# Gated linear attention inside a full decoder layer: the running sums of the gate made by a VectorE scan instead of fp32 products with a triangle of ones

## The reference, cut to what matters

```python
log_a = log_sigmoid((za @ w_gla_gate + b_gla_gate)) / 16        # (tokens, 4 heads * 128 channels)
# per chunk of tokens and per head:
cum = jnp.cumsum(gc, axis=-2)                                   # running sum of log_a over the tokens
o_inter = einsum('ik,kv->iv', qc * exp(cum), state)
attn    = (qc * exp(cum)) . (kc * exp(-cum)), causal            # written out with a decay in the reference
o_intra = einsum('ij,jv->iv', attn, vc)
state   = state * exp(last)[:, None] + (kc * exp(last - cum)).T @ vc
```

## Time and profile before

| | us |
|---|---|
| median of 3 runs | 2958.1 |
| the runs | 2984.66, 2958.1, 2953.07 |
| the profiled execution | 2954.94 |
| its span, slowest core (core 0) | 2953.4 |
| spans of the other cores | 2937.2 to 2952.8 |
| PE busy | 2800.8 (95%) |
| DVE busy | 1564.1 (53%) |
| ACT busy | 1341.3 (45%) |
| mean granted TensorE clock, core 0 | 0.986 |

### The profile page before, as it was taken

One profiled execution on the slowest core, in us unless ns is written; L12 is line 12 of the kernel. 1 busy time (PEld: TensorE's weight loads), 2 busy tenths in 40 slices (PEclk: granted clock), 3 DMA queues, 4 the chain that ended last, 5 costly groups with the idle time before them and its releaser, 6 DMA issues.

```text
span 2953.4 us, 47945 instructions; the slowest of 8 cores (2937.2 to 2953.4 us)
## 1 busy us (share of the span) xinstructions
PE 2800.8 (95%) x16320; PEld 1413.5 (48%) x16627; DVE 1564.1 (53%) x2490; ACT 1341.3 (45%) x2678; POOL 757.7 (26%) x980
## 2 busy tenths in 40 slices
PE   6999999997989997799999999999999999999998
PEld 2454455664545554344444455554444444444443
DVE  5887666664434443344454455445564554554643
ACT  4776565554665564222332265443442442433421
POOL 4665787774444454200001000000000000000000
PEclk9999999998999999899999999999999999999999
DMA  7774565886433436655556588978512113113121
GB/s 143 165 166 93 91 100 80 110 113 93 58 65 61 69 73 105 176 124 131 143 141 152 125 198 188 187 179 224 149 52 79 54 52 95 47 58 97 29 65 50
DMA packets 392398, 323.47 MB, mean 110 GB/s; under 512 B 282262, under 2 KB 335822, under 8 KB 391694
## 3 DMA queue, kind: packets, MB, share of 16 engines
q1 hardware_dynamic: 330382, 218.86, 30.6%
q0 software_dynamic: 61408, 101.36, 19.6%
q10 hardware_dynamic: 368, 0.16, 0.0%
HBM read 219.83 MB, written 108.92 MB: 111 GB/s over the span
## 4 chain that ended last, share of the span: by engine, by line
PE 84%; DMA 5%; DVE 4%; issue 3%; ACT 3%; POOL 1%; DVEq 0%; SPq 0%; ACTq 0%; POOLq 0%
PE psum_all L252 83%; DMA oa_d<-B1b_on 3%; DMA C_wd<-w_in 1%; DVE C_s L321 1%; ACT C_pP L278 1%; ACT L278 1%; DVE B1b_on L311 1%; POOL B1b_Sbf L303 1%; DVE C_pP L285 0%; DVE C_qkb L285 0%; DMA T1Ap_obt<-T1Ap_ob 0%; PE psum_all L256 0%; DVE C_oe L317 0%; ACT C_s L278 0%; DMA T_x<-T2hi_xs 0%
## 5 line engine op out<-in xcount | busy, mean ns | idle before, releaser
L252 PE MATMUL psum_all<-T_x,T_wup 128*128 128x512 bf16 x2759 | 605.9, 379 | 3.0
L252 PE MATMUL psum_all<-C_wd,xnT 128*128 128x512 bf16 x2212 | 541.3, 386 | 26.8 <-DMA C_wd<-w_in 13.2
L252 PEld LDWEIGHTS psum_all<-T_x,T_wup 128*128 128x128 bf16 x2816 | 275.4, 98 | 332.4
L252 PEld LDWEIGHTS psum_all<-C_wd,xnT 128*128 128x128 bf16 x2304 | 252.4, 121 | 210.6 <-issue 25.5
L311 DVE SCALAR_TENSOR_TENSOR T_c<-psum_all,T2hi_wcb,T_c 128x511 f32<-128x511 f32 x352 | 263.4, 748 | 168.4 <-ACT T_c L278 150.0
L252 PE MATMUL psum_all<-T_wdn,T_yT 128*128 128x512 bf16 x1381 | 303.8, 379 | 1.4
L252 PE MATMUL psum_all<-xnT,T1A_wmg 128*128 128x512 bf16 x1004 | 233.8, 384 | 6.7 <-DVE B1b_on L311 5.6
L252 PEld LDWEIGHTS psum_all<-T_wdn,T_yT 128*128 128x128 bf16 x1408 | 137.8, 98 | 166.1
L278 ACT ACT_TABLE_LOAD x134 | 171.9, 1283 | 77.6 <-DVE T1A_mT L285 32.6
L285 DVE TENSOR_TENSOR C_pP<-C_pP,C_mask 128x1024 bf16<-128x1024 bf16 (+1 forms) x192 | 127.3, 663 | 129.9 <-ACT C_pP L278 129.9
L316 ACT COPY T2hb_hist<-psum_all 128x2 f32<-128x2 f32 x154 | 24.2, 157 | 378.3 <-PE psum_all L252 378.1
(11 more groups left out here) (217 smaller groups left out, 4279.7 us busy)
## 6 DMA issues: line engine op xcount, KB each, us to landing
T2hi_h<-h_d SPq DMA_DIRECT2D x40, 512.0 KB, 4.6
og_d<-C_oe POOLq DMA_DIRECT2D x64, 260.0 KB, 4.9
C_xt<-x SPq DMA_DIRECT2D x32, 512.0 KB, 5.4
T1Ah_xt<-x POOLq DMA_DIRECT2D x32, 512.0 KB, 10.1
h_d<-T1Ah_xt SPq DMA_DIRECT2D x32, 512.0 KB, 3.8
T1B_h1x<-h_d SPq DMA_DIRECT2D x32, 512.0 KB, 5.1
h_d<-T1B_h1x SPq DMA_DIRECT2D x32, 512.0 KB, 6.4
out<-T2hi_h SPq DMA_DIRECT2D x21, 512.0 KB, 3.0
```

What stands on the lines that cost most here:

```text
L252: return self._add("pe", lambda e: e.matmul(o, l, r, start=start, stop=stop), [lhsT, rhs], [out], xr=xr)
```

## The change

The gate is made turned: the operands of the four matmuls of `P_a2` are exchanged, so that each `sp` tile holds one head's 128 channels on the partitions and the 512 tokens of the supertile along the row. A new DVE instruction, a scan (`tensor_tensor_scan`), then runs along the 512 tokens in place: state = fresh[t] * state + sp[t], where the constant tile `fresh` is 1.0 but for 0.0 at the first token of each chunk, so the sum starts anew there. The result is what the fp32 matmuls with the triangle put into PSUM; `P_b` reads it from the `sp` tile, and its fp32 matmuls and their PSUM bank are gone. `za` has one buffer in place of two, which gives its space to `fresh`.

```diff
+    def scan(self, out, data0, data1, initial, op0, op1):
+        o, a, b = out.ap, data0.ap, data1.ap
+        return self._add("dve", lambda e: e.tensor_tensor_scan(o, a, b, initial, op0, op1), [data0, data1], [out])
...
-        zar = Rot([sb(st, "za%d" % i, (33, 512), BF16) for i in range(2)])
+        zar = Rot([sb(st, "za%d" % i, (33, 512), BF16) for i in range(1)])
...
+        fresh = sb(st, "fresh", (128, 512), BF16)
+        fw.memset("dve", fresh[:, :], 1.0)
+        fw.memset("dve", fresh[:, 0:512:128], 0.0)
...
-            for c4 in range(4):
+            for h in range(4):
                 pz = PB.next()
-                fw.mm(pz[:, :], za[:, c4 * 128:(c4 + 1) * 128], wgg[:, :])
+                fw.mm(pz[:, :], wgg[:, h * 128:(h + 1) * 128], za[:, :])
                 e1 = e1r.next()
                 fw.act(e1[:, :], pz[:, :], AF.Exp, scale=-1.0)
-                fw.act(spb[c4][:, :], e1[:, :], AF.Ln, bias=one_c, scale=1.0)
+                fw.act(spb[h][:, :], e1[:, :], AF.Ln, bias=one_c, scale=1.0)
+
+                fw.scan(spb[h][:, :], fresh[:, :], spb[h][:, :], 0.0, ALU.mult, ALU.add)
...
-                pc = PB.next()
-                for c4 in range(4):
-                    fw.mm(pc[:, c4 * 128:(c4 + 1) * 128], spb[c4][:, h * 128:(h + 1) * 128], cst[:, 1, :])
+                pc = spb[h]
```

## The result

The changed kernel takes 2985.4 us as the median of ten runs beside 2956.3 for the kernel before on the same chip. By the comparable runs the ratio is 1.0078, 95% interval 1.0042 to 1.0114: slower by 0.8%, clear of the noise by that interval and less than the 1% that the prediction counts as no change. Some executions of all these kernels ran with a whole die at a lower clock; the ratios leave them out, and of e6, whose trace is such a one, only the other die (cores 4 to 7) is read.

What follows compares the result with a forecast made beforehand. PE, busy 378.5 of the loop's 400 us, was taken as the bound. Removal -23.8 and -4.4, scans +31.0 and clock +10.4 give +13.2 on 2954.9; with 1 added for the median, 2969 us, range 2946 to 2982.

Steps and rivals of the forecast that it cites:

- Removal, loop: Steps c4 = 2 and 3 of seven supertiles: PE loses the fp32 groups, 3.40 us a supertile, -23.8 us.
- The step that looked ahead for the next thing to be late: Step c4 = 3: DVE's `ke` chain limits the gain to 1.62 us in place of 1.78.
- Start: First supertile, prepared before the loop: four fp32 groups gone, less 0.2 for scans ahead of attention masks, -4.4 us.
- The scans: Step c4 = 1, between `on` and the mask: four scans of 1.20 us delay PE's restart, +31.0 us over seven supertiles.
- The upper bound: Scan's price on DVE: a two-operation instruction over 1024 elements, 1.28 us, 1.20 from start to start.
- The clock: Behind PE's longer waits in step c4 = 1: granted clock falls, 6 x 2.0 - 1.6 = +10.4 us, bounds 0 and 15.9.
- At nothing: No cost from turned matmuls, ACT reading `sp` in SBUF, `P_b`, memsets, the freed PSUM bank, single `za`, or later stages.
- The sum: Whole kernel: removal, start, scans and clock together, +13.2 us on the profiled execution's 2954.9, 2968.1.
- the first: Rival: scans on DVE keep one element a turn, 0.60 us each; -7 us, 2948 us; chance 0.17.
- the second: Rival: PE's clock stays high through the longer waits, scan at 1.20; +3 us, 2958 us; chance 0.10.
- the third: Rival: scans 0.3 us dearer each and all seven waits pay 2.5 for the clock; +27 us, 2982 us; chance 0.07.
- the fourth: Rival: PE's freed time goes into other waits; 11 us lost if step c4 = 3's `ke` takes all, 2980 us; chance 0.06.

Runs made afterwards that it cites:

- e6: The changed kernel with three buffers for `on` in place of two, and two `at` masks in place of three; ratio 0.9948 to the kernel before.
- e1: The changed kernel with the loop's scans issued behind the mask and v copy of step c4 = 1, not ahead of them; 2930.0 us.
- e4: The changed kernel with each scan replaced by an elementwise product of the same two tiles; ratio 1.0009 to the kernel before.
- e5: The changed kernel with 16 unread matmuls of 512 columns added on PE in its wait of step c4 = 1; ratio 1.002 to the kernel before.
- e9: The kernel before with three buffers for `on` and two `at` masks, no scans; median 2943.7 us.
- e10: The changed kernel without the scans, with three buffers for `on` and two `at` masks; 2916.1 and 2919.2 us in two comparable runs.
- e2: The changed kernel with the scan line removed, so the running sums are left out; 2932.8 us.
- e3: The kernel before, fp32 products kept, with 32 scans added at the change's place, results unread; ratio 1.0177 to the kernel before.
- e7: The changed kernel with the loop's scans behind the mask and v copy, three buffers for `on` and two `at` masks; 2911.9 us.
- e8: The changed kernel with each scan followed by a second one into a scratch tile; ratio 1.0164 to the kernel before.

## Why the prediction was right, and where not

Right was the mechanism and its sign: PE's freed work is outweighed because the scans stand between `on` and the mask, and the clock adds to it. The two runs without a stretch at 0.81, 2970.6 and 2971.7, are 2 us from 2969. e1 settles the place, e4 the length, e5 the clock. By its steps:

- **Removal, loop: -23.8.** Measured -22.7: -24.0 of PE's work (28 groups at 0.86; 0.89 between e9 and e10) and +1.3 in wait ke. The step that looked ahead for the next thing to be late was right in kind and took 1.1 for it. What it missed is the DMA behind it: with PE earlier, `on` waits longer for its buffer, and `qe` and `ke` stand behind it on DVE. In all, wait ke grows by 1.3 here, and by 4.1 and 3.8 in e1 and e2, where nothing else holds PE back.
- **Start: -4.4.** Measured -4.3.
- **The scans: +31.0.** Measured +27.7 in after and +31.0 in e3. The upper bound was the right one to take: 1.205 us for 1.28. From start to start it is 1.12, not 1.20, so four cost 4.47, not 4.80, and `on` to restart is 8.73 for 9.06. By the prediction's own sum that takes 2.2 off the 31.0 (28 x 0.08). It doesn't explain the 27.7 by itself: in e3 `on` to restart is 8.73 too, and wait v grows by the full 31.0, so hitting that number there is in part luck. Why e3 pays more than after isn't traced; the forecast started from one core's waits, 10.1 us, and the cores of before lie between 4.3 and that. In the first supertile PE's wait is 3.17 us on core 2, 2.7 over the 0.45 of the earlier trace rows, where 2.8 was put.
- **The rule cited for the scan** (the Trainium skill, DVE: opcode table, instruction layouts, handler registers and perf-mode slots, "Datapath and trigger behaviour": half throughput) agrees with the trace: 1205 ns beside e4's 686 for the same shape, and 1.12 us from start to start beside 0.60 in the earlier trace rows.
- **The clock: +10.4.** This is the term that was mis-sized: +14.4. Six times 2.0 less 1.6 was put; it is seven times 2.2 less 0.8. The windows at 0.50 to 0.68 are those that it named, but the first supertile's wait of 3.2 us, which it left out, pays too (1.2 to 1.7 us on cores 2 to 7), and the others average more than its 2.0, between 0.9 and 3.0 each. The bound of 15.9 held. It rested on one window behind one wait: in the same trace the second supertile's wait of 3.00 us, as long as the 2.97 that it read, is followed by windows at 1.00, so waits of 3 us may or may not bring the clock down. The window behind that restart, core 0 of before:

```profile
825.00:830.00 5.00, 4.94 (x32) 3.27 (x34) 1.66 (x4) 4.82 (x12) 2.45 (x2) 1.00 0.01 3
```

- **At nothing.** ACT: scans waited 1.8 us in all for `sp`, PE never. Stages behind the loop: each moved by 1.1 us at most. The single `za`: no wait for its buffer.
- **The sum: +13.2.** On cores without the stretch at 0.81 it is -22.7 - 4.3 + 27.7 + 14.4 = +15.1. The clock's +4 and the removal's +1 are nearly paid by the scans' -3.3, so part of the closeness is luck.
- **The median.** That of all ten runs is 2985.4, 3 over the range's end; that of the seven comparable ones is 2981.7, just inside it. What lifts it, cores with a stretch at 0.81, was not foreseen. It is no term of the change's own account, but after shows it in five of these seven runs.

Of the rivals, e4 shows what the first would have been (2952, put at 2948), and e5 comes close to the second (2960, put at 2958). Both were priced well and ruled out for the right reason. Of the third, the scan stayed under the upper row (1.205 for 1.28), but all seven waits pay for the clock, as it had it: 15.2 in all, where it put 17.5. Of the fourth, PE's freed time lost to `ke`, 1.3 of the 11 us came. The prediction asked only whether the scans can go ahead of `on`. That they can go behind the copy, where DVE is idle, it didn't ask, and that was worth 41 us.

## What to carry to other kernels

Moving work to an engine with room is worth what stands behind it in that engine's queue: find the last instruction that the bound engine waits for, and put the new work behind it, not ahead. When PE stops waiting at one place, look at what now comes early against a buffer that a DMA still empties; one more buffer gave about 14 us before the change and 18 on top of the moved scans (e9, e7 against e1). Price a longer wait of PE with the clock that it brings down, here 1.2 to 2.2 us for each as a mean, and split the loop into waits, clock and rest before believing in a term.

## What the runs showed of the hardware

- A running sum of 512 fp32 elements takes 1205 ns, an elementwise product over the same tiles 686 ns. An independent scan starts about 0.08 us before the end of the one ahead in the records, one that reads its output 0.1 us after.
- The cost of PE's wait in granted clock is not proportional to it. As a mean it is 1.2 us for waits of 3.2 to 3.5 us (e6), 2.2 for waits of 5 us (after) and 2.2 again for 8.2 to 12.8 us (e8). Single waits scatter: nothing behind 3.00 us and 1.6 behind 2.97 on one core of before, 0.9 to 3.0 behind 4.2 to 6.4 us in after.
- Some cores have a long stretch at a granted clock of 0.81, neither of the two levels (0.50 and 1.00): on core 1 of after every window of 5 us from 775 to 930 is at 0.81, but for three behind restarts (0.50, 0.71 and 0.60). The same core in long windows (busy times, then clock):

```profile
760.00:800.00 40.00, 36.01 (x157) 16.69 (x156) 19.29 (x33) 18.98 (x42) 14.40 (x17) 0.84 0.42 60
800.00:900.00 100.00, 91.30 (x391) 40.78 (x388) 43.16 (x76) 53.35 (x117) 41.56 (x43) 0.79 0.30 53
900.00:935.00 35.00, 33.84 (x142) 15.47 (x143) 14.97 (x28) 16.41 (x38) 14.37 (x17) 0.78 0.33 61
940.00:960.00 20.00, 19.48 (x102) 8.90 (x99) 9.01 (x19) 15.29 (x36) 13.59 (x13) 1.00 0.37 79
```

The matmuls bear it out (duration ns least, median, most; first and last start). Core 1 inside the stretch, then core 2 over its whole trace:

```profile
L252 PE MATMUL psum_all<-xnT,B_wqk x159: 435/437/634, 785.5 to 929.7; 128*128 128x512 bf16 x159
```

```profile
L252 PE MATMUL psum_all<-xnT,B_wqk x512: 379/379/634, 715.7 to 1154.3; 128*128 128x512 bf16 x171
```

The stretch makes the loop of cores 0 and 1 14 and 21 us longer than that of the others (426.6 and 433.5 for 412.9), and with it the kernel. In after it begins behind the first restart at a lower clock. Where a trace shows it, it comes in pairs of cores: 0 and 1 in after, 4 and 5 in e3. In e6's trace cores 0 and 1 have it from about 45 to 1435 us, and cores 2 and 3 from about 1885 to the end, so it isn't bound to the restarts of the loop, and the two pairs of a die have it at different times. In runs without a trace the longer spans are not always those of two cores: all four of a die are longer in one run each of after (2986.0), e3 (3018.4) and e4 (2981.6), three in one of e5 (2979.5). No comparable run of e1, e6, e7 or e9 stands so far above its others, one of six or eight does in e4 and e5, and a few of before do (2963.9, 2968.4, 2984.7). That it comes more often with PE's waits of 5 us is a count over few runs, e8 with longer waits has none in three, and its cause stays open. The Trainium skill (TensorE: Matmul & The Clock Gate, "Seeing it yourself") tells of a peak-current limit that takes the clock to 13/16, 0.81, but on a whole die and while the load lasts. The level agrees. The reach doesn't: in after cores 2 and 3 are of the same die and have windows at 1.00 in the same stretch, and cores 0 and 1 are back at 1.00 in the middle of the loop; in e6 two cores of a die are at 0.81 while the other two are at 1.00.
